# A mixture of 16,384 experts: rows gathered per token, or every expert for every token as dense matmuls

## The reference, cut to what matters

```python
def peer(h, w_pq, pk1, pk2, pu, pv):
    n = h.shape[0]
    q = (h @ w_pq).reshape(n, P_HEADS, 2, P_HALF).astype(jnp.float32)
    s1 = jnp.einsum('nhd,hkd->nhk', q[:, :, 0], pk1.astype(jnp.float32))
    s2 = jnp.einsum('nhd,hkd->nhk', q[:, :, 1], pk2.astype(jnp.float32))
    v1, i1 = lax.top_k(s1, P_TOPK)
    v2, i2 = lax.top_k(s2, P_TOPK)
    cand = (v1[..., :, None] + v2[..., None, :]).reshape(n, P_HEADS, P_TOPK * P_TOPK)
    cidx = (i1[..., :, None] * P_NKEYS + i2[..., None, :]).reshape(n, P_HEADS, P_TOPK * P_TOPK)
    sc, j = lax.top_k(cand, P_TOPK)
    e = jnp.take_along_axis(cidx, j, axis=-1)
    g = jax.nn.softmax(sc, axis=-1)
    ue = pu[e]
    ve = pv[e]
    a = jax.nn.gelu(jnp.einsum('nhkd,nd->nhk', ue, h).astype(jnp.float32), approximate=False)
    return jnp.einsum('nhk,nhkd->nd', (g * a).astype(h.dtype), ve)
```

## Time and profile before

| | |
|---|---|
| three runs | 4867.93, 4873.79, 4850.75 us; median 4867.93 |
| span of the profiled execution, first to last instruction | 4854.9 us |
| the median of the runs less that span | 13.0 us |
| TensorE, VectorE, GpSimd, ScalarE busy | 78%, 53%, 50%, 17% of the span |
| moved over DMA | 1185 MB, 1108 MB of it gathered |

### The profile page before, as it was taken

How to read it: one execution, slowest core, us unless ns; L and a number is a source line. 1 busy time by engine, 2 the same in 40 slices (tenths; PEclk the granted TensorE clock), 3 DMA queues, 4 the chain that set the end, 5 groups by cost and what they waited for, 6 DMA issues and landing times.

```text
span 4854.9 us, 35025 instructions
## 1 busy us (share of the span) xinstructions
PE 3808.4 (78%) x10196; PEld 1735.7 (36%) x10196; DVE 2587.8 (53%) x5932; ACT 821.8 (17%) x1886; POOL 2443.7 (50%) x2256
## 2 busy tenths in 40 slices
PE   9899898878999667888676667677778667667677
PEld 4444445545664523333222222223234222222222
DVE  0323239997214675666565465465556656445453
ACT  1210123332100111111111111111111111111111
POOL 0000000000000077777777777777777777777776
PEclk9889989987799889999999999999999999999999
DMA  2100100000210499999999999999999999999998
GB/s 82 36 2 2 55 19 20 14 7 1 70 35 27 128 340 347 354 333 332 355 364 363 366 367 360 367 372 362 362 364 388 352 355 355 359 359 353 352 368 320
DMA packets 405562, 1185.00 MB, mean 244 GB/s; under 512 B 39936, under 2 KB 125248, under 8 KB 405264
## 3 DMA queue, kind: packets, MB, share of 16 engines
q0 software_dynamic: 304384, 1107.96, 61.2%
q1 hardware_dynamic: 101008, 74.99, 5.1%
HBM read 1176.60 MB, written 6.20 MB: 244 GB/s over the span
## 4 chain that ended last, share of the span: by engine, by line
POOL 20%; DMA 17%; PE 15%; issue 9%; DVE 5%; ACT 1%; POOLq 0%; DVEq 0%; SPq 0%; ACTq 0%
DMA v_rows<-in_pv,v_rows_at 14%; PE acc L1412 11%; POOL u_rows L1351 10%; POOL v_rows L1357 9%; PE pq_ps L1379 4%; DMA u_rows<-in_pu,u_rows_at 2%; DVE u_rows L1614 1%; PE key_ps L1387 0%; DVE key_at L1507 0%; DVE one_hot L1600 0%; ACT diag L1461 0%; DVE one_hot L1596 0%; DVE key_top L1504 0%; DVE top_at L1507 0%; DVE expert_f L1602 0%
## 5 line engine op out<-in xcount | busy, mean ns | idle before, releaser
L1412 PE MATMUL acc<-v_rows,diag 128*128 128x512 f32 (+1 forms) x4224 | 2064.5, 623 | 840.6 <-DMA v_rows<-in_pv,v_rows_at 587.5
L1614 DVE CUSTOM_DVE_ANT_0 u_rows<-u_rows,late 128x1024 f32<-128x1024 f32 x1056 | 1274.2, 1226 | 1061.5 <-DMA u_rows<-in_pu,u_rows_at 1054.7
L1412 PEld LDWEIGHTS acc<-v_rows,diag 128*128 128x128 f32 (+1 forms) x4224 | 751.2, 192 | 2135.1 <-issue 1261.4
L1357 POOL DMA_INDIRECT v_rows<-in_pv,v_rows_at x1056 | 1225.1, 1160 | 325.3 <-issue 235.8
L1351 POOL DMA_INDIRECT u_rows<-in_pu,u_rows_at x1056 | 1179.8, 1117 | 369.9 <-issue 291.3
L1461 ACT ACTIVATE diag<-ident_sb,expert_w 128x128 f32<-128x128 f32 x1024 | 379.7, 397 | 1451.4 <-PE acc L1412 1364.6
L1338 POOL COPY u_rows_at<-expert 128x16 uint32<-128x16 uint32 (+1 forms) x66 | 20.2, 306 | 1193.2 <-DVE expert L1605 1180.8
L1379 PE MATMUL pq_ps<-xT_sb,w_pq_sb 128*128 128x256 f32 (+2 forms) x768 | 238.8, 465 | 8.2 <-DMA iota_sb<-in_iota 7.6
L306 POOL DMA_DIRECT2D out_gla_p<-gla_S x4 | 2.3, 587 | 480.9 <-DVE gla_S L630 480.9
L1504 DVE MAX8 key_top<-key_scores 128x8 f32<-128x128 f32 (+1 forms) x288 | 68.1, 283 | 271.2 <-ACT key_scores L1447 171.3
L930 DVE MAX8 m<-score 128x8 f32<-128x384 f32 (+6 forms) x209 | 183.4, 878 | 5.3
(11 more groups left out here) (207 smaller groups left out, 3045.9 us busy)
## 6 DMA issues: line engine op xcount, KB each, us to landing
w_pq_sb<-in_w_pq SPq DMA_DIRECT2D x48, 512.0 KB, 12.6
u_rows<-in_pu,u_rows_at POOLq DMA_INDIRECT x1056, 6.2
v_rows<-in_pv,v_rows_at POOLq DMA_INDIRECT x1056, 6.2
xT_sb<-in_xT SPq DMA_DIRECT2D x8, 528.0 KB, 7.0
w_gvr<-in_w_in SPq DMA_DIRECT2D x2, 2048.0 KB, 13.0
w_gk<-in_w_in SPq DMA_DIRECT2D x8, 512.0 KB, 6.1
w_dsa<-in_w_in SPq DMA_DIRECT2D x2, 2048.0 KB, 10.3
w_b<-in_w_in SPq DMA_DIRECT2D x8, 512.0 KB, 4.2
```

Source lines behind the costliest of these rows:

```text
L1357: pool.indirect_dma_start(out=V[:, j % RING, :], out_offset=None, in_=io["pv"], in_offset=bass.IndirectOffsetOnAxis(ap=atv[:, b, j:j + 1], ...
L1412: last = pe.matmul(acc[0:R, c * 512:(c + 1) * 512], dg[:, j % DG, 0:R], V[:, j % RING, c * 512:(c + 1) * 512], start=False, stop=False)
L1614: dve.tensor_tensor_reduce(U[:, j % RING, :], U[:, j % RING, :], h1[:, t, :], 1.0, 0.0, ALU.mult, ALU.add, dots[:, b, j:j + 1]).then_inc(d ...
```

## The change

`run_experts` no longer gathers. It goes through all experts for all tokens in two passes, and the passes hand over two arrays in DRAM that the kernel makes for itself.

Pass 1 goes over 128 blocks of 128 experts (`EB`). SP loads a block of `pu`, TensorE transposes it (`turn`, eight transposes, ScalarE copies them back), and multiplies it with all tokens (`product`, three pieces of 352 tokens, eight matmuls each). ScalarE takes gelu of the sums, and SP stores them as `gelu_rows`. Beside the first 17 blocks TensorE also makes queries and key scores, for all tokens at once (`query`, `keys`), and VectorE takes the best 16. From block 24 on (`FIRST`) a dense matrix of weights is built, three quads of four tokens beside each block: TensorE turns a tile's chosen keys and weights so that a token's 128 choices lie on the partitions (`turn_chosen`), GpSimd compares a row of counts with the first key (`oh1`), VectorE with the second and multiplies by the weight (`hot_quad`), and one matmul of 128x128 a token adds all its choices up (`weights`). ScalarE copies a quad to `stage`; after eight quads SP stores 32 tokens' matrix, 2 MB, as `weight_rows`. VectorE picks for the next tile between the quads.

Pass 2 goes over 32 groups of four blocks, three times, for three token tiles each time (`PASSES`). SP loads gelu and weights of the pass's tokens (the latter in runs of 512 bytes) and 2 MB of `pv`; VectorE multiplies the first two (`coefficients`); TensorE adds the product with `pv` to the sums of the three tiles, which stay in PSUM over the 32 groups, 24 matmuls of 512 columns a group. `finish` adds the tokens and normalises, in the next pass or at the end.

```diff
--- before.py
+++ after.py
+    EB = NEXP // P
     NB = 2 * PH
-    NS = PH * PK * TS // P
+    TC = [(0, 352), (352, 704), (704, 1056)]
+    QUADS = [r // 4 for r in ROWS]
+    NQ = sum(QUADS)
+    QAT = [sum(QUADS[:t]) for t in range(TILES)]
+    NG = NT // 32
+    KT = [[0, 1, 2, 3], [4, 5, 6, 7], [8]]
+    FIRST = 24
+    gelu_rows = nc.dram_tensor("gelu_rows", (EB, P, NT), F32, kind="Internal").ap()
+    weight_rows = nc.dram_tensor("weight_rows", (NG, P, P * 32), F32, kind="Internal").ap()
+    def quads_beside(c):
+        return [q for q in range(3 * (c - FIRST), 3 * (c - FIRST) + 3) if 0 <= q < NQ]
...
-        U = sb("u_rows", [P, RING, D])
-        V = sb("v_rows", [P, RING, D])
...
+                def load_block(c):
+                    if c >= 3:
+                        sp.wait_ge(turned, 2 * (c - 3) + 2)
+                    sp.dma_start(pu[:, c % 3, :], puv[c]).then_inc(pu_in[c % 3], 16)
...
+                for c in range(EB):
+                    if c + 2 < EB:
+                        load_block(c + 2)
+                    if 1 <= c and c + 1 < NB:
+                        load_query(c + 1)
+                    if c >= 1:
+                        sp.wait_ge(gelu_done, 3 * c)
+                        sp.dma_start(gelu_rows[c - 1], ga[:, (c - 1) % 3, :]).then_inc(ga_out[(c - 1) % 3], 16)
+                    while stored < NG and 8 * stored + 8 <= 3 * (c - 1 - FIRST):
+                        sp.wait_ge(w_copied, 8 * (stored + 1))
+                        sp.dma_start(weight_rows[stored], stage[:, stored % 2].rearrange("p c n -> p (c n)")).then_inc(stage_out[stored % 2], 16)
+                        stored += 1
...
+                def turn(c, half):
+                    if half == 0:
+                        pe.wait_ge(pu_in[c % 3], 16 * (c // 3 + 1))
+                    if c:
+                        pe.wait_ge(turned_copied, 2 * (c - 1) + half + 1)
+                    for b in range(4):
+                        last = pe.transpose(tps[:, half, b * P:(b + 1) * P], pu[:, c % 3, (4 * half + b) * P:(4 * half + b + 1) * P], ident[:])
+                    last.then_inc(turned, 1)
+                def product(c, s):
+                    n, (a, b) = 3 * c + s, TC[s]
+                    if s == 0:
+                        pe.wait_ge(turned_copied, 2 * c + 2)
+                    if n >= 2:
+                        pe.wait_ge(gelu_done, n - 1)
+                    for kk in range(KD):
+                        last = pe.matmul(sps[:, n % 2, 0:b - a], puT[:, c % 2, kk, :], h1T[:, kk, a:b], start=(kk == 0), stop=(kk == KD - 1))
+                    last.then_inc(s_ready, 1)
...
+                def turn_chosen(t):
+                    R = ROWS[t]
+                    pe.wait_ge(sel_ready, t + 1)
+                    pe.wait_ge(k_copied, 3 * NB)
+                    if t:
+                        pe.wait_ge(sel_copied, t)
+                    for x in range(3):
+                        last = pe.transpose(kps[:, x * P:x * P + R], sel[0:R, t % 2, x, :], ident[0:R, 0:R])
+                    last.then_inc(sel_turned, 1)
+                def weights(q):
+                    pe.wait_ge(hot1_built, q + 1)
+                    pe.wait_ge(hot2_built, q + 1)
+                    if q >= 2:
+                        pe.wait_ge(w_copied, q - 1)
+                    for x in range(4):
+                        last = pe.matmul(gps[:, q % 2, x * P:(x + 1) * P], oh2[:, q % 4, x, :], oh1[:, q % 4, x, :], start=True, stop=True)
+                    last.then_inc(w_ready, 1)
...
+                turn(0, 0)
+                turn(0, 1)
+                for c in range(EB):
+                    if c + 1 < EB:
+                        turn(c + 1, 0)
+                    if c == FIRST - 2:
+                        turn_chosen(0)
+                    for s in range(3):
+                        if c < NB:
+                            query(c, s)
+                        if 1 <= c <= NB:
+                            keys(c - 1, s)
+                        product(c, s)
+                        if s == 0 and c + 1 < EB:
+                            turn(c + 1, 1)
+                        for q in quads_beside(c)[s:s + 1]:
+                            weights(q)
+                            t = tile_of(q)
+                            if t + 1 < TILES and q == QAT[t] + 28:
+                                turn_chosen(t + 1)
...
+                def copy_weights(q):
+                    k = q // 8
+                    act.wait_ge(w_ready, q + 1)
+                    if k >= 2 and q % 8 == 0:
+                        act.wait_ge(stage_out[k % 2], 16 * (k // 2))
+                    act.copy(stage[:, k % 2, :, 4 * (q % 8):4 * (q % 8) + 4],
+                             gps[:, q % 2, :].rearrange("p (x c) -> p c x", x=4)).then_inc(w_copied, 1)
...
-                            pool.indirect_dma_start(out=U[:, j % RING, :], out_offset=None, in_=io["pu"],
...
+                for t in range(TILES):
+                    pool.wait_ge(sel_copied, t + 1)
+                    for q in range(QAT[t], QAT[t] + QUADS[t]):
+                        if q >= 4:
+                            pool.wait_ge(w_ready, q - 3)
+                        for x in range(4):
+                            n = 4 * (q - QAT[t]) + x
+                            last = pool.tensor_scalar(oh1[:, q % 4, x, :], count[:], selT[:, t % 2, 0, n:n + 1], None, ALU.is_equal)
+                        last.then_inc(hot1_built, 1)
...
-                        dve.tensor_tensor_reduce(U[:, j % RING, :], U[:, j % RING, :], h1[:, t, :], 1.0, 0.0, ALU.mult, ALU.add,
...
+                def hot_quad(t, q):
+                    if q >= 4:
+                        dve.wait_ge(w_ready, q - 3)
+                    for x in range(4):
+                        n = 4 * (q - QAT[t]) + x
+                        last = dve.tensor_scalar(oh2[:, q % 4, x, :], count[:], selT[:, t % 2, 1, n:n + 1], selT[:, t % 2, 2, n:n + 1],
+                                                 ALU.is_equal, ALU.mult)
+                    last.then_inc(hot2_built, 1)
+                for part in range(PH + 2):
+                    pick(0, part)
+                for t in range(TILES):
+                    dve.wait_ge(sel_copied, t + 1)
+                    for q in range(QAT[t], QAT[t] + QUADS[t]):
+                        hot_quad(t, q)
+                        part, left = divmod(q - QAT[t], 2)
+                        if t + 1 < TILES and left == 1 and part <= PH:
+                            pick(t + 1, part)
+                        if t + 1 < TILES and q == QAT[t] + 24:
+                            pick(t + 1, PH + 1)
+    GRP = EB // 4
+    PASSES = [(0, 1, 2), (3, 4, 5), (6, 7, 8)]
+    AT = [(0, 384), (384, 768), (768, NT)]
...
+                pvv = io["pv"].rearrange("(g c p) d -> g p c d", c=4, p=P)
+                gav = gelu_rows.rearrange("(g c) p n -> g p c n", c=4)
+                wtv = weight_rows.rearrange("k p (g c) -> g p k c", c=P)
+                for m in range(3 * GRP):
+                    p, g = divmod(m, GRP)
+                    a, b = AT[p]
+                    if m >= 4:
+                        sp.wait_ge(block_done, m - 3)
+                    sp.dma_start(ca[:, m % 4, :, 0:b - a], gav[g, :, :, a:b]).then_inc(ca_in[m % 4], 16)
+                    if m >= 3:
+                        sp.wait_ge(c_ready, 4 * (m - 2))
+                    sp.dma_start(wt[:, m % 3, 0:(b - a) // 32].rearrange("p k c n -> p k (c n)"), wtv[g, :, a // 32:b // 32]).then_inc(wt_in[m % 3], 16)
+                    sp.dma_start(V[:, m % 4], pvv[g]).then_inc(V_in[m % 4], 16)
...
+                for m in range(3 * GRP):
+                    p, g = divmod(m, GRP)
+                    pe.wait_ge(c_ready, 4 * (m + 1))
+                    pe.wait_ge(V_in[m % 4], 16 * (m // 4 + 1))
+                    for i, t in enumerate(PASSES[p]):
+                        R = ROWS[t]
+                        if g == 0 and t >= 4:
+                            pe.wait_ge(added, t - 3)
+                        for h in range(2):
+                            for c in range(4):
+                                last = pe.matmul(ops[0:R, t % 4, h * 512:(h + 1) * 512], ca[:, m % 4, c, i * P:i * P + R], V[:, m % 4, c, h * 512:(h + 1) * 512],
+                                                 start=(g == 0 and c == 0), stop=(g == GRP - 1 and c == 3))
+                        if g == GRP - 1 and i < 2:
+                            last.then_inc(o_ready, 1)
+                    last.then_inc(block_done, 1)
...
+                def coefficients(m, c):
+                    a, b = AT[m // GRP]
+                    if c == 0:
+                        dve.wait_ge(ca_in[m % 4], 16 * (m // 4 + 1))
+                        dve.wait_ge(wt_in[m % 3], 16 * (m // 3 + 1))
+                    x = ca[:, m % 4, c, 0:b - a].rearrange("p (k n) -> p k n", n=32)
+                    dve.tensor_tensor(x, x, wt[:, m % 3, 0:(b - a) // 32, c, :], ALU.mult).then_inc(c_ready, 1)
...
```

(61 more changed lines are left out.)

497 lines of the change are left out of this document (193 added, 304 removed).

## The result

The changed kernel takes 6073.84 us (median of four executions, 6055.0 to 6076.98) beside 4868.31 us for the kernel before in the same comparison: ratio 1.2465, 95% interval 1.243 to 1.2501, 24.6% slower. The forecast was 6060 us, with a range of 6020 to 6180. The profiled execution took 6055.0 us.

What follows compares the result with a forecast made beforehand. The old experts' stage was taken as gather-bound, the new one as bound by TensorE's fp32 matmuls: 1592 + 13 + 2425 + 3.5 + 26 + 1977 + 10 = 6046.5 us, plus 13 us, so 6060 us; range 6020 to 6180.

Steps and rivals of the forecast that it cites:

- The price of a matmul: TensorE's fp32 matmul, start to start: two records, 0.592 us at 352 columns and 0.858 us at 512.
- Rival (c): Both passes: new matmuls cost one record, so products, queries, keys and weights halve; some 3915 us in all; chance 0.02.
- Entry: Start of the experts: first loads 10.8 us plus 2.4 us of half clock, together 13 us.
- Pass 1: TensorE over 128 blocks: 2425 us; a block 15.1 us, 31.3 with query and keys, 17.7 with weights.
- the wait at block 22: Pass 1: TensorE waits once for exponent and normalisation before turning the first tile's chosen lists, 3.5 us.
- Between the passes: Last gelu and its store, first loads of pass 2, 2.4 us of half clock: 26 us, TensorE mostly idle.
- Pass 2: 96 steps of 24 matmuls of 512 columns on TensorE: 1977 us, 20.6 a step, third pass no cheaper.
- Tail: The last tile's normalisation at the kernel's end: 10 us, from 9.1 us in the kernel before.
- The 13 us added at the end: Whole kernel: the median of the runs lies 13 us above the profiled span, added to the sum.
- What lies beside it: Pass 1: ScalarE, VectorE, DMA and GpSimd stay hidden behind TensorE; GpSimd's comparison at 0.6 us, hidden below 1.48 us.

Runs made afterwards that it cites:

- e7: The changed kernel with pass 1's products and pass 2 in fp16, queries, keys and choice of experts left fp32: 3758.34 us, ratio 0.7742 to the gathering kernel.
- e6: The changed kernel with only pass 2's operands rounded to fp16, DMA traffic unchanged: 5037.38 us, ratio 1.0365 to the gathering kernel.
- e1: The changed kernel run again unaltered, as a base for other runs: 6078.27 us.
- e3: The changed kernel with each GpSimd comparison made twice, the extra one into an unread buffer: 6069.46 us.
- e4: The changed kernel with each GpSimd comparison made three times, the extra two into an unread buffer: 6463.1 us.
- e9: e7 with gelu and the dense weights also stored as fp16 in scratch DRAM: 3613.01 us, ratio 0.7397 to the gathering kernel.

## Why the prediction was right

**The price of a matmul** decided it: two records, 0.592 and 0.858 us. Rival (c), one record for an fp32 matmul, did not come true. That cheaper matmuls turn the sign does: e7, where a product of either pass costs one record and a quarter of the time, is faster than the gathers. That its 3758 us lie near the 3915 worked out for (c) is chance, since that sum halves every matmul and lets nothing else bind, while in e7 queries, keys and weights keep their price and GpSimd and transfers bind. The Trainium skill's formula (TensorE: Matmul & The Clock Gate, "Back-to-back issue gap"), given there for an isolated matmul, makes 149 ns for 352 columns and 216 ns for 512. It agrees with fp16 matmuls in a row: 0.149 us in e7's products, 0.216 us at the median in e6's pass 2. For fp32 the four passes that the Trainium skill gives (FP8 and Floating Point Precision, "TensorE Precision Notes") agree with 0.592 us, four times 0.149.

**The sum, term by term**, from the first query to the end, is 4454.4 us in the profiled execution against some 4444 forecast. That it is so near is in part luck, for errors of 8 to 12 us in three terms partly cancel:

- Entry: the first query at 1598.85 us, 10.2 us after the first issue (1588.61), and 7.30 us for 16 records that later take 4.90. Together 12.6; 13 forecast (the 2.4 us lie in the next stretch too, and are counted once in the sum). The granted clock was 0.50 up to 1603 us, that is 1.2 GHz, and 1.00 from 1604.
- Pass 1: 2439 us to the last product, with the wait at block 22; forecast 2431 (2425, 3.5 and 2.4 of the entry's half clock). The wait was 3.18 us, near the 3.5 priced, but it had a price behind it that I left out: from 2201 to 2204 us the granted clock was 0.50, and the next 16 records took 6.59 us for 4.90. Most of the other 7 us lie in the blocks with queries: their first transposes stand 31.60 us apart for 31.3, some 5 us in sixteen blocks. The blocks with weights, 17.76 us for 17.73, add 2 to 3. Why a block with queries takes 0.3 us more was not tested.
- Between the passes: TensorE idle for 16.6 us, then 1.5 us more in the first step of pass 2 than in those behind it (granted clock 0.50 up to 4057 us). That is 18.1 us against 26 forecast, of which 2.4 were for the clock. I had taken the store at 6.6 us, and the page has 2.9 for `gelu_rows`; I had taken 16 for the loads at the rate of `w_out`, and the first matmul came 12.95 us after the first load's issue at 4041.93.
- Pass 2: 1989 us, 1977 forecast. Records follow each other by 0.429 us as in the earlier trace rows. The 1.5 us of the first step are in it, and the steps with the 32-token tile took 20.92 us, not 20.6, which is 10 us over 32 steps. The prediction said that the third pass is no cheaper; it is dearer, and what of the smaller tile costs the 0.3 us a step was not tested.
- Tail: 9.1 us after 6044.11; 10 forecast.

**The 13 us added at the end** were misread. I took them for something around the span. The profiled execution took only 1.8 us more than its span, while the median of the four lies 20.6 us above that span. What differs between executions is when the experts begin: the first query came at 1597.3 to 1631.8 us in the table, while the part behind it repeats within 2 us in the kernels that keep it. The windows of the first 600 us show a lower clock in the late one, e1 (0.89 and 0.83 in 0 to 200 and 200 to 600) than in the early one (0.94 and 0.87). All ten profiles of the table fit: from 0 to 1590 us the clock is 0.88 in the five whose first query came by 1604 us, and 0.86 or 0.87 in the five that were later. That the clock causes all 33 us was not tested. So the term's size is the middle of a spread, not a cost that every execution pays.

**What lies beside it** held: GpSimd's comparison took 0.602 us at the median (0.6 taken, between 0.295 and 2.36), VectorE's one-hot 0.344 (0.99 as bound); GpSimd's 688 ns on the page are the mean. GpSimd's cover is measured by e3 and e4: one more such operation is free, two are not. VectorE's and ScalarE's cover was not tested so, but in the window of the blocks with weights they were busy 455 and 302 of 1200 us.

## What to carry to other kernels

Price a dense rewrite by the matmul's own start-to-start time at its data type before counting bytes saved: here halved traffic bought nothing in fp32, because TensorE's 4402 us stood against a gather stage of 3260. In fp16 the same rewrite won. When the bound is removed, expect the covered ones in turn (here GpSimd at 12 comparisons a block and DMA at 10 us a step), and find their floors by doubling and tripling them while they are still covered. Compare profiled executions from a common event behind the noisy stages; that took the spread of the unaltered work from 33 us to under 2.

## What was not expected of the hardware

- A scattered write by ScalarE cost nothing extra: the copy of the dense weights, 512 columns written in another order, took 586 ns, the same as the plain copy.
- Loads with runs of 512 bytes (the dense weights, a fifth of a step's bytes) beside longer ones ran at 350 to 369 GB/s, and with 256 bytes (e9) still at 348.
- GpSimd's comparison of 128 columns, 0.602 us, is only twice its copy of 16.
- In e6 and e7 the granted clock fell to 0.84 in pass 2, where TensorE waited for `pv` and its copy. No run holds the clock at 1.00 there, so its cost is not known.
